# Closing loads behind the last expert block, and the opening of layer 1 in two groups of tiles

## The reference, cut to what matters

```python
for l in range(DEPTH):
    need_ctx = l < DEPTH - 1
    hl = _layer_norm(xl) * (1.0 + sc1) + sh1
    hc = _layer_norm(xc) * (1.0 + csc1) + csh1
    yl, yc = _token_mixing(hl, hc, need_ctx, ...)
    xl = _layer_norm(alpha * xl + g1 * yl, ln1_g[l], ln1_b[l])
    ...
    ml = _expert_choice_ffn(_layer_norm(xl) * (1.0 + sc2) + sh2, ...)
    xl = _layer_norm(alpha * xl + g2 * ml, ln2_g[l], ln2_b[l])      # the closing
    # the context: the same, in layer 0 only
return xl
```

## Time and profile before

| | |
|---|---|
| median of 3 runs | 3628.44 us (3627.48 to 3639.15) |
| profiled execution, its own time | 3626.51 us |
| its span | 3624.5 us |
| TensorE busy | 3313.7 us, 91% of the span |
| VectorE, ScalarE, POOL busy | 62%, 46%, 19% |
| mean granted clock of TensorE | 0.959 of full speed |
| moved from and to HBM | 630.76 MB, 174 GB/s on the mean |

### The profile page before, as it was taken

The page is one execution under the profiler, slowest core; times in us unless marked ns, Lnnn a source line. Parts: engine busy times, 40 slices in busy tenths (PEclk is TensorE's granted clock), DMA queues, the critical chain, the costliest instruction groups (busy, mean ns, idle before and its releaser), DMA issues.

```text
span 3624.5 us, 49898 instructions
## 1 busy us (share of the span) xinstructions
PE 3313.7 (91%) x19060; PEld 2798.6 (77%) x19060; DVE 2247.2 (62%) x3354; ACT 1683.0 (46%) x2169; POOL 686.3 (19%) x486
## 2 busy tenths in 40 slices
PE   7999889899999979999998399898999969999995
PEld 4987569799999857777776388677888857877884
DVE  3685861521221649999998584742313448999997
ACT  3113752522221247777775622753322127777774
POOL 3001012223222011221221200012244201111111
PEclk9989999999999989999999699998999979999998
DMA  7364024013222339999998144121132219999995
GB/s 257 95 167 119 11 62 150 24 47 103 90 82 73 109 121 334 334 326 338 338 328 319 66 112 92 33 74 47 47 111 93 94 70 309 358 340 354 358 362 211
DMA packets 446036, 630.76 MB, mean 174 GB/s; under 512 B 130910, under 2 KB 221454, under 8 KB 439470
## 3 DMA queue, kind: packets, MB, share of 16 engines
q1 hardware_dynamic: 309056, 557.88, 44.6%
q0 software_dynamic: 20336, 63.25, 5.3%
q10 hardware_dynamic: 116480, 7.35, 2.2%
HBM read 611.90 MB, written 23.84 MB: 175 GB/s over the span
## 4 chain that ended last, share of the span: by engine, by line
PE 62%; DVE 17%; issue 7%; ACT 7%; DMA 6%; ACTq 0%; POOL 0%; DVEq 0%; SPq 0%; POOLq 0%
PE ps L906 41%; PE ps L1340 10%; DVE part L2296 4%; DMA raw<-in_w_exp_gate 3%; PE ps L1046 2%; DVE hx L2296 2%; DVE area L1883 2%; DVE area L2304 2%; PE ps L1078 2%; DMA raw<-in_w_exp_down 1%; ACT hx L1677 1%; PE ps L1064 1%; ACT area L1516 1%; PE ps L1066 1%; ACT area L1402 1%
## 5 line engine op out<-in xcount | busy, mean ns | idle before, releaser
L906 PE MATMUL ps<-hx,part 128*128 128x384 f32 (+2 forms) x5088 | 968.1, 350 | 11.8 <-POOL part L566 5.5
L906 PEld LDWEIGHTS ps<-hx,part 128*128 128x128 f32 x5088 | 877.2, 189 | 99.0 <-issue 8.7
L1340 PE MATMUL ps<-part,hx 128*128 128x512 f32 x3072 | 747.3, 395 | 19.8 <-ACT part L1677 9.7
L1340 PEld LDWEIGHTS ps<-part,hx 128*128 128x128 f32 x3072 | 571.9, 189 | 153.5 <-issue 11.8
L2296 DVE TENSOR_TENSOR part<-raw,part 128x2048 fp32r<-128x2048 f32 x256 | 597.8, 2336 | 32.6 <-ACT part L1677 31.1
L1677 ACT ACTIVATE part<-raw 128x2048 fp32r<-128x2048 f32 x256 | 490.3, 1916 | 162.8 <-DMA raw<-in_w_exp_up 75.4
L566 POOL TENSOR_TENSOR part<-raw,part 128x2048 fp32r<-128x2048 f32 x68 | 314.5, 4625 | 743.9 <-ACT part L563 741.9
L1340 PE MATMUL ps<-hx 128*128 128x512 f32 x1536 | 384.4, 399 | 13.0 <-ACT hx L1677 8.1
L1340 PEld LDWEIGHTS ps<-hx 128*128 128x128 f32 x1536 | 288.9, 190 | 90.1 <-ACT hx L1677 11.8
L2296 DVE TENSOR_TENSOR hx<-raw,hx 128x2048 fp32r<-128x2048 f32 x128 | 293.6, 2294 | 48.0 <-ACT hx L1677 46.6
L563 ACT ACTIVATE part<-raw 128x2048 fp32r<-128x2048 f32 x92 | 175.7, 1911 | 277.2 <-PE ps L906 159.9
(11 more groups left out here) (287 smaller groups left out, 3677.3 us busy)
## 6 DMA issues: line engine op xcount, KB each, us to landing
raw<-in_w_exp_gate SPq DMA_DIRECT2D x128, 1024.0 KB, 6.2
raw<-in_w_exp_up SPq DMA_DIRECT2D x128, 1024.0 KB, 6.7
raw<-in_w_exp_down SPq DMA_DIRECT2D x128, 1024.0 KB, 6.7
raw<-in_w_mod SPq DMA_DIRECT2D x48, 1024.0 KB, 6.7
raw<-in_w_in SPq DMA_DIRECT2D x44, 1024.0 KB, 5.5
raw<-in_w_gate SPq DMA_DIRECT2D x32, 1024.0 KB, 5.4
raw<-in_w_branch SPq DMA_DIRECT2D x16, 1024.0 KB, 5.2
raw<-in_w_out SPq DMA_DIRECT2D x8, 1024.0 KB, 4.9
```

The costliest lines, as they stand in the source:

```text
L906: last = mm(dst, a, b, start=i == 0, stop=i == len(pairs) - 1)
L1340: last = mm(ps[:, bank, :], x, y, start=kh == 0 and a == 0, stop=kh == 1 and a == len(pairs) - 1)
```

## The change

POOL gets a wait, before the closing loads, for the ring slot of the last expert block of the layer. The load of row 1 of `rows2` (the context's gate) is made only in layer 0, and the last stage waits for three rows instead of four.

In the opening of layer 1, the loops of ScalarE and VectorE run over two groups of tiles, (0 to 3) and (4, 5), one after the other. TensorE transposes the four latent tiles (`turn_tile`), starts the first group of matmuls of the convolution, transposes tile 4 after it and tile 5 after the second. In layer 1 the convolution uses banks 4 to 7 (`conv_bank`) instead of 0, 2, 4 and 6; the first gate group waits for all second deviations, and the wait for all of h stands ahead of the attention projections. The low parts of the first two blocks are written by VectorE instead of POOL: the first after `close_sum` of tile 0, the second after the first group. Layer 0's opening is as it was, but for the place of POOL's `mixers_to`.

```diff
@@ -500,6 +500,10 @@
+        def conv_bank(l, j, gate):
+
+            return 4 * (1 - j % 2) + 2 * gate if l == 0 else 4 + j % 2 + 2 * gate
+
         def conv_parts(l):
@@ -708,7 +712,6 @@
                 if l:
-                    split.mixers_to(l, 2)
                     for t in range(NT):
@@ -718,8 +721,7 @@
                     store_mod(0)
-                split.mixers_to(l, 2)
-                if l == 0:
+                    split.mixers_to(l, 2)
                     stored(0)
@@ -856,9 +858,12 @@
                 pool.wait_ge(*S("xg", l).at(2 * E))
+                last = B_EXP[l] + EXP_BLOCKS * E - 1
+                pool.wait_ge(ring_in[last % RING], 16 * (last // RING + 1))
                 for v, src in enumerate((mod_d[l, 0:1, 5 * D:6 * D], mod_d[l, 1:2, 5 * D:6 * D],
                                          A["ln2_g"][l:l + 1, :], A["ln2_b"][l:l + 1, :])):
-                    load(rows2[:, v, :], src.to_broadcast([P, D])).then_inc(*S("rows2_in", l).by(16))
+                    if v != 1 or full == NT:
+                        load(rows2[:, v, :], src.to_broadcast([P, D])).then_inc(*S("rows2_in", l).by(16))
                 for t in range(full):
@@ -957,7 +962,7 @@
-                for t in range(NT):
+                def turn_tile(t):
                     if l:
@@ -966,6 +971,9 @@
                     last.then_inc(*S("xhat_T", l).by(1))
+
+                for t in range(TL if l else NT):
+                    turn_tile(t)
                     if l == 0 and t < 2:
@@ -979,10 +987,16 @@
                                 pe.wait_ge(*S("conv_glu", l).at(j - 1))
-                            if j == 1 and not gate:
+                            if l == 0 and j == 1 and not gate:
                                 pe.wait_ge(*S("h_done", l).at(NT))
-                            feature_major(4 * (1 - j % 2) + 2 * gate, w, j % 2 * P, toks, (TL, NT) if j + gate == 0 else ()
+                            if l and j + c == 0 and gate:
+                                pe.wait_ge(*S("v_std", l).at(NT))
+                            feature_major(conv_bank(l, j, gate), w, j % 2 * P, toks, (TL, NT) if j + gate == 0 else ()
                                           ).then_inc(*pa.by(ORD[l]["in", S_CONV + 2 * c + gate], j % 2))
+                            if l and c + gate == 0:
+                                turn_tile(TL + j)
+                if l:
+                    pe.wait_ge(*S("h_done", l).at(NT))
@@ -1420,28 +1434,29 @@
                     split.mixers_to(l, 2)
-                    for s in range(NT + 3):
-                        if s >= 3:
-                            modulated(s - 3)
-                        if 1 <= s <= NT:
-                            act.wait_ge(*S("x2", l).at(s))
-                            deviation(s - 1, 6, 10, 7, S("v_std", l))
-                        if 2 <= s <= NT + 1:
-                            t, sf = s - 2, stat[:, (s - 2) % 4, :]
-                            act.wait_ge(*S("v_nb", l).at(t + 1))
-                            if t >= 2:
-                                act.wait_ge(*S("xhat_T", l).at(t - 1))
-                            fn(xhat2[:, t % 2, :], x2v[:, t, :], ACT.Identity, bias=sf[:, 9:10], scale=sf[:, 8:9]
-                               ).then_inc(*S("xhat_n", l).by(1))
-                        if s < NT:
-                            closing(s, 0)
+                    for ta, tb in ((0, TL), (TL, NT)):
+                        for s in range(ta, tb + 3):
+                            if s >= ta + 3:
+                                modulated(s - 3)
+                            if ta + 1 <= s <= tb:
+                                act.wait_ge(*S("x2", l).at(s))
+                                deviation(s - 1, 6, 10, 7, S("v_std", l))
+                            if ta + 2 <= s <= tb + 1:
+                                t, sf = s - 2, stat[:, (s - 2) % 4, :]
+                                act.wait_ge(*S("v_nb", l).at(t + 1))
+                                if t >= 2:
+                                    act.wait_ge(*S("xhat_T", l).at(t - 1))
+                                fn(xhat2[:, t % 2, :], x2v[:, t, :], ACT.Identity, bias=sf[:, 9:10], scale=sf[:, 8:9]
+                                   ).then_inc(*S("xhat_n", l).by(1))
+                            if s < tb:
+                                closing(s, 0)
...
                         act.wait_ge(*S("conv_glu", l).at(j))
-                    b = 4 * (1 - j % 2) + 2
+                    b = conv_bank(l, j, 1)
                     last = fn(csg[:, 0:LAT], ps[:, b, :], ACT.Sigmoid)
@@ -1831,28 +1846,33 @@
                         low_part(u)
-                else:
+                split = Split(dve, "lo", V)
+                if l:
                     dve.wait_ge(*S("rows2_in", l).at(0))
                     dve.wait_ge(*S("x1_in", l).at(0))
-                    for s in range(NT + 3):
-                        if 1 <= s <= NT:
-                            own(close_norm(s - 1, 0))
-                            negative_mean(stat[:, (s - 1) % 4, :], 5, 6).then_inc(*S("x2", l).by(1))
-                            dve.wait_ge(*S("x2", l).at(s))
-                        if 2 <= s <= NT + 1:
-                            sf = stat[:, (s - 2) % 4, :]
-                            dve.wait_ge(*S("v_std", l).at(s - 1))
-                            own(V.reciprocal(sf[:, 8:9], sf[:, 7:8]))
-                            own.wait()
-                            V.tensor_tensor(sf[:, 9:10], sf[:, 6:7], sf[:, 8:9], ALU.mult).then_inc(*S("v_nb", l).by(1))
-                        if s == 2:
-                            take_modt(0, 4).then_inc(*S("modc_done", l).by(1))
-                        if s < NT:
-                            close_sum(s, 0)
-                        if s >= 3:
-                            low_part(s - 3)
-
-                split = Split(dve, "lo", V)
+                    split.mixers_from(l, 0)
+                    for ta, tb in ((0, TL), (TL, NT)):
+                        for s in range(ta, tb + 3):
+                            if ta + 1 <= s <= tb:
+                                own(close_norm(s - 1, 0))
+                                negative_mean(stat[:, (s - 1) % 4, :], 5, 6).then_inc(*S("x2", l).by(1))
+                                dve.wait_ge(*S("x2", l).at(s))
+                            if ta + 2 <= s <= tb + 1:
+                                sf = stat[:, (s - 2) % 4, :]
+                                dve.wait_ge(*S("v_std", l).at(s - 1))
+                                own(V.reciprocal(sf[:, 8:9], sf[:, 7:8]))
+                                own.wait()
+                                V.tensor_tensor(sf[:, 9:10], sf[:, 6:7], sf[:, 8:9], ALU.mult).then_inc(*S("v_nb", l).by(1))
+                            if s == 2:
+                                take_modt(0, 4).then_inc(*S("modc_done", l).by(1))
+                            if s < tb:
+                                close_sum(s, 0)
+                            if s >= ta + 3:
+                                low_part(s - 3)
+                            if s == 0:
+                                split.mixers_to(l, 1)
+                        split.mixers_to(l, 2)
+
                 segs = [(0, 0, LAT), (LSEG, LAT, CTX)] if ctx_out else [(0, 0, LAT)]
@@ -1861,7 +1881,7 @@
                     dve.wait_ge(*S("conv_sig", l).at(j + 1))
-                    b = 4 * (1 - j % 2)
+                    b = conv_bank(l, j, 0)
                     last = V.tensor_tensor(cpad[:, j, HALO:HALO + LAT], ps[:, b, :], csg[:, 0:LAT], ALU.mult)
@@ -1883,7 +1903,8 @@
                 dve.wait_ge(*S("conv_zero", l).at(1))
-                split.mixers_from(l, 2)
+                if l == 0:
+                    split.mixers_from(l, 2)
                 split.mixers_to(l, 3)
@@ -2369,7 +2390,7 @@
                 if l == DEPTH - 1:
-                    dve.wait_ge(*S("rows2_in", l).at(64))
+                    dve.wait_ge(*S("rows2_in", l).at(48))
                     dve.wait_ge(*S("x1_in", l).at(16 * full))
```

## The result

The changed kernel takes 3602.82 us (median of 4 runs, 3600.1 to 3609.56), the kernel before, on the same chip, 3629.91 us. The ratio is 0.993, with a 95% interval from 0.9915 to 0.9945: faster, by 25.4 us (20.0 to 30.9), about as much as forecast (3605). The profiled execution took 3609.56 us, with a span of 3607.5; it is the slowest of the four.

A forecast was written before the change was run, and what follows sets the result against it. TensorE, busiest by far, was taken as the bound, so only its idle or slow stretches give time back. Closing loads 18.6 us plus opening 3.9 us made 22.5 us; forecast 3605 us, range 3598 to 3615.

The forecast's parts named there:

- The last experts: Last expert of each layer: with closing loads held back it runs like earlier ones, gaining 10.4 and 10.9 us.
- rival C: Last experts: slow by themselves, not through the closing loads; 3627 us, chance 0.07.
- Rival D: Both stage ends: the loads' landing becomes the wait that sets them, 36 us lost against 25.2 gained; 3639, chance 0.04.
- layer 1's loads: End of layer 1: seven closing loads take 13.6 of 15.6 us, so they are hidden with 2 us to spare.
- The closing loads of layer 0 late: End of layer 0: the loads land too late for VectorE's first instruction of layer 1; 2.7 us lost, bounds 0 and 7.
- released by a DMA: Sign at layer 1's start: a DMA releases VectorE's first instruction, some 2 to 3 us after the stage's end.
- Rival B: End of layer 0: closing loads are in time, POOL's queue getting a larger share beside SP's blocks; 3602, chance 0.12.
- POOL's splits gone: Layer 1's opening: moving POOL's two weight-block splits to VectorE gains 7.7 us.
- the start of the convolution at 48.7 us: Layer 1's opening: convolution can begin 48.7 us after the opening's start instead of 68.1, 19.4 us earlier.
- What is given back: Layer 1's opening: TensorE waits for tile 4; projections 63.9 us after convolution's start, at 112.6 against 116.5, gain 3.9 us.
- Rival A: Layer 1's opening gives nothing: passes 1 and 2 at the lower clock, split in the way; 3609 to 3611, chance 0.15.
- The second rise: Layer 1's opening: TensorE's clock rises again in pass 2 after the wait; a rise costs 1.5 us.

The follow-up runs named there:

- e2: The kernel before with only the closing part: closing loads wait for the last weight block, layer 1 opens as before; ratio 0.9949.
- e3: The changed kernel with only the new opening: closing loads go out where they did before; ratio to the kernel before 0.9986.
- e5: The changed kernel, with POOL's arrival at the stage's end put ahead of its closing loads; ratio to the kernel before 0.9924.
- e6: e5, with VectorE waiting for the tiles by three semaphores, each where it first uses one; ratio to the kernel before 0.9913.
- e4: The changed kernel with all six tiles in one group, all transposes ahead of the convolution, VectorE's splits kept; ratio to the kernel before 0.9928.
- e1: The changed kernel itself, unchanged, run again for a second trace; ratio to the kernel before 0.9939.
- e7: e4, with one pass of the convolution between the transposes of tile 4 and tile 5; ratio to the kernel before 0.9926.
- e11: The changed kernel once more, timed beside e9 and e10; 3604.53 us, ratio to the kernel before 0.9933.
- e8: e6 and e7 together; median 3594.3 us, ratio to the kernel before 0.9908.
- e10: The kernel of e8 once more, timed beside e9 and the changed kernel; 3595.67 us, ratio to the kernel before 0.991.
- e9: e8, with VectorE's second split put ahead of tile 4's low part; 3594.9 us, ratio to the kernel before 0.9909.

## Why the prediction was right

**The last experts**, 10.4 and 10.9 us forecast: right, 11.0 and 10.5 (other runs up to 11.0 in layer 1). e2 and e3 show that the loads were the cause; rival C falls. Rival D falls too: layer 1's loads landed 2.4 us ahead of their use (2 forecast).

**The closing loads of layer 0 late**, 2.7 us forecast: the loads were late as worked out, but I named the wrong waiter and the term was too small, 4.9 us. I looked for VectorE's first instruction "released by a DMA"; it was released by POOL's queue. I had put POOL's leaving of the stage behind its loads and written that "nobody waits for POOL before all engines leave", which left out that POOL can leave only when its own loads have landed. The forecast had VectorE at 13.1 + 2.7 = 15.8 us; it came at 18.05. Of the 2.25 us between, 1.0 is a later start (first issue 7.0 us before the landmark, 8.0 forecast), 0.6 slower landing (1959.33 to 1983.4, 24.1 us for 23.5), and the rest, some 0.6 us, the drain's end and the meeting of the engines where I had 0.2. e5 and e6 tell the two waits apart: the drain gone, 16.9; VectorE's wait for all tiles gone too, 14.7. What is left over the 13.1 of before is a fall of TensorE's clock (last section). Rival B had 3602, nearer to the 3602.82 measured than the forecast is, but its mechanism is not there: the loads were late. It falls.

**POOL's splits gone**, 7.7 us forecast, and **the start of the convolution at 48.7 us**: measured 48.70. Both terms held. With the splits gone (e4) the fourth tile's h was complete 50.00 us after VectorE's start instead of 57.94, 7.9 us earlier; with the deviation of tile 4 left out it was complete after 48.55, 1.45 us earlier again (1.5 forecast).

**What is given back**: forecast, the projections 63.9 us after the convolution's start, measured 61.5 (2094.54 - 2033.04). TensorE did wait for tile 4 until 16.8 us after it (17.0 forecast). Behind the wait I had 2.0 + 7.0 + 1.7 us up to the gates, and it was 8.7 (2049.82 to 2058.56): the transposes overlap with the pass behind them (their starts are 1.6 and 0.8 us apart, where I had 2.0 and 1.7), and the pass took 6.49. So the opening gave 6.3 us in this run and 5.1 to 6.5 over all kernels with two groups, against 3.9 forecast: a term of the sum mis-sized by 2.4 us. Rival A falls. The granted clock, in windows at pass 1's start, and over tile 4, pass 2 and tile 5:

```profile
2033.00:2035.00 2.00, 1.96 (x5) 1.60 (x6) 2.00 (x1) 0.00 (x0) 0.00 (x0) 0.50 0.00 0
...
2049.80:2058.00 8.20, 8.18 (x35) 6.97 (x36) 1.22 (x1) 5.10 (x10) 1.92 (x3) 0.80 0.23 72
```

The second rise is there (0.80 on average behind the wait), as the rule of the Trainium skill that the prediction drew on (TensorE: Matmul & The Clock Gate, "Loop structure matters more than you think") has it; the trace agrees, and e4 gives the price of two groups with all their effects, 2.0 to 3.4 us.

The two errors in the sum, 2.2 us too little lost at the end of layer 0 and 2.4 too little gained in the opening, cancel: 22.5 forecast, 22.9 by the landmarks. That the total was closer than its steps is luck.

## What to carry to other kernels

Where full DMA engines feed the critical path, small prefetches for the next stage can cost a great deal (here 4 to 5 MB beside the 12 MB of an expert cost over 10 us in each layer); issue them behind the last block that is urgent, but then look at what leaves the stage: an engine that drains behind its own loads holds every engine until they land. Let it arrive first and let the user wait for each piece where it is used (3.4 us here). Before splitting a loop so that TensorE can start earlier, count the time at which its last piece is ready: here a start 11 us earlier cost 2 to 3 us in the end, and one pass set into a gap, with its weights ready, gained 6 us.

## What the runs showed of the hardware

POOL's drain ended only when the loads on its own queue had landed, 19.4 us after the end of its last issue, while it had no other work. The drain ended 0.6 us after the last landing in this run, and so it did in e1, e2, e4, e7 and e11, whose last landings lay at other distances (17.5 to 19.4 us from the issue). With the arrival ahead of the loads (e5) the stage no longer waited for it.

TensorE's clock after one and the same idle stretch of 2.25 to 2.26 us, between the last expert's products and the 16 matmuls that scatter its rows, fell to 0.50 in some executions and not in others. The changed kernel in its first run, TensorE's row of the timeline and the window behind its start:

```profile
1970.62 5.53 PE L911 MATMUL ps<-hx 128*128 128x512 f32 x16 [2.26 <-DVE hx L2364]
```

```profile
1972.00:1974.00 2.00, 2.00 (x6) 1.53 (x5) 1.52 (x3) 0.00 (x0) 0.00 (x0) 0.50 1.01 422
```

The same kernel in e11, the same two views:

```profile
1971.55 4.04 PE L911 MATMUL ps<-hx 128*128 128x512 f32 x16 [2.26 <-DVE hx L2364]
```

```profile
1972.00:1974.00 2.00, 2.00 (x11) 1.61 (x10) 1.69 (x3) 0.00 (x0) 0.00 (x0) 1.00 1.00 414
```

After the first runs I took this for an effect of the late loads, since before and e3 did not have it and all others did; e7, e8 and e11 have the late loads and no fall, which disproves that. In all it fell in 8 of 13 executions: in two of three of the changed kernel, and in one of two of the kernel of e8 and e10. It costs 1.5 us where the stage's end hangs on it: e8 ends at 13.17 without it, e6, e9 and e10 at 14.66 to 14.72 with it. What decides it is open.

The loads of POOL's queue and SP's blocks together moved 422 and 414 GB/s in these two windows, and SP's blocks nearly by themselves 350 to 355 in the experts of layer 1, with the DMA engines' share at 1.00 to 1.01 in both. Why full engines moved more in the one than in the other is open.
